# Dealing an expert's ranks to the partitions in steps of eight

## What is computed

```
pg   = softmax(h @ wg);  g_sel = argmax(pg)                 # 4 groups
pf   = softmax of the chosen group's 8 expert logits
top_p, top_i = top_k(pf, 2)                                 # two experts of that group
wts  = max(pg) * top_p / sum(top_p)
out  = sum over the token's two experts of  wts * W_down(silu(W_gate h) * W_up h)
```

## Time and profile before

| | us |
|---|---|
| runs shown | 1400.77, 1408.01, 1413.49 |
| median of the runs | 1408.01 |
| span of the profiled execution | 1406.2 |
| TensorE busy in it | 1299.9 (92%) |
| mean granted TensorE clock | 0.962 |

### The profile page before, as it was taken

How to read it: one execution, slowest core, us unless ns; L and a number is a source line. 1 busy time by engine, 2 the same in 40 slices (tenths; PEclk the granted TensorE clock), 3 DMA queues, 4 the chain that set the end, 5 groups by cost and what they waited for, 6 DMA issues and landing times. The chain is left out here.

```text
span 1406.2 us, 19509 instructions
## 1 busy us (share of the span) xinstructions
PE 1299.9 (92%) x6977; PEld 927.7 (66%) x6977; DVE 743.2 (53%) x1444; ACT 263.0 (19%) x564; POOL 278.5 (20%) x397
## 2 busy tenths in 40 slices
PE   7999999999999999999989888999999799787775
PEld 3787767878778777777777776888878533222224
DVE  1625688998877777100136558675666612111116
ACT  3201112222222443110222213400002300000001
POOL 0223433423334343131200002000002301111000
PEclk9999999999999999999999997999999899999995
DMA  9553233431331334665541113322244599999945
GB/s 362 178 112 113 89 101 120 150 117 64 120 120 60 120 136 141 212 206 166 166 183 35 31 31 136 124 60 90 89 171 193 220 419 419 420 419 420 419 202 200
DMA packets 66594, 250.88 MB, mean 178 GB/s; under 512 B 9834, under 2 KB 21770, under 8 KB 53290
## 3 DMA queue, kind: packets, MB, share of 16 engines
q1 hardware_dynamic: 49858, 213.34, 40.3%
q0 software_dynamic: 10112, 20.47, 4.3%
q10 hardware_dynamic: 6536, 15.90, 3.9%
HBM read 234.47 MB, written 22.91 MB: 183 GB/s over the span
## 5 line engine op out<-in xcount | busy, mean ns | idle before, releaser
L362 PE MATMUL psum<-arena 128*128 128x272 f32 x2408 | 568.9, 394 | 6.4 <-DVE arena L2331 2.0
L362 PEld LDWEIGHTS psum<-arena 128*128 128x128 f32 x2408 | 452.9, 190 | 118.4 <-issue 19.9
L384 POOL TENSOR_TENSOR arena<-arena 128x512 f32<-128x512 f32 x96 | 128.0, 1333 | 202.7 <-DMA arena<-in_weights 158.9
L2840 PE MATMUL psum<-arena 128*64 128x512 f32 x512 | 119.2, 611 | 21.4 <-DMA arena<-in_w_gu 19.0
L1507 PE MATMUL psum<-arena 128*128 128x272 f32 x512 | 121.6, 395 | 0.0
L1507 PEld LDWEIGHTS psum<-arena 128*128 128x128 f32 x512 | 95.3, 189 | 25.1 <-DVE arena L1633 3.6
L2840 PEld LDWEIGHTS psum<-arena 128*64 128x64 f32 x512 | 36.2, 138 | 93.7 <-issue 70.3
L2862 PE MATMUL psum<-arena 128*64 128x512 f32 x256 | 65.1, 654 | 18.9 <-issue 16.2
L2914 DVE TENSOR_TENSOR arena<-arena,psum 128x256 f32<-128x256 f32 x16 | 6.8, 422 | 131.3 <-ACT arena L2905 131.3
L1633 DVE TENSOR_TENSOR arena<-arena,psum 128x272 f32<-128x272 f32 x16 | 7.0, 438 | 128.2 <-ACT arena L1584 128.2
L1827 PE MATMUL psum<-arena 128*128 128x272 f32 x256 | 63.8, 403 | 3.0 <-PEq L206 3.0
(11 more groups left out here) (390 smaller groups left out, 1517.6 us busy)
## 6 DMA issues: line engine op xcount, KB each, us to landing
arena<-in_weights SPq DMA_DIRECT2D x153, 512.0 KB, 4.7
arena<-in_w_gu SPq DMA_DIRECT2D x32, 2048.0 KB, 34.5
arena<-in_w_down SPq DMA_DIRECT2D x16, 2048.0 KB, 34.9
arena<-in_weights ACTq DMA_DIRECT2D x16, 512.0 KB, 4.6
arena<-in_pages_k POOLq DMA_DIRECT2D x40, 128.0 KB, 3.7
arena<-in_x SPq DMA_DIRECT2D x2, 2176.0 KB, 11.9
arena<-in_pages_v SPq DMA_DIRECT2D x32, 128.0 KB, 3.3
arena<-in_pages_v POOLq DMA_DIRECT2D x32, 128.0 KB, 3.5
```

Of the source, the lines that this page charges most:

```text
L362: mm = pe.matmul(out, lhsT=w[:, c * P:c * P + P], rhs=x[:, c, :], start=(c == 0 and not added), stop=(c == 3), skip_group_check=added or more)
L384: link(dve.tensor_tensor(sums[:, k], a, b, op))
L2840: mm = pe.matmul(psum[CAP * e:CAP * e + CAP, 2 + k, :].rearrange("p (o f) -> p o f", o=2), lhsT=xgT[:, k, lo:lo + CAP], rhs=wv[:, e, c4], ...
```

## The change

The slot that a rank gets is no longer the rank itself. The 64 slots are seen as 8 groups (b) of 8 (a), and slot 8b + a gets rank 8a + b: rank 0 goes to partition 0, rank 1 to 8, rank 2 to 16, rank 7 to 56, rank 8 to 1, and so on, in both halves of the partitions. The table of rows, the table of weights and all that follows use the same `slot_of`, so each token still meets its expert. It is one instruction, with another view of its first operand and of its output; it runs once before the pairs and once behind them.

```
+SLOT_STEP = 8
 ...
                 def one_hot_slots():
-                    dve.tensor_tensor(slot_of, const("iota").unsqueeze(1).to_broadcast([P, 2 * NR, CAP]),
-                                      rank.unsqueeze(2).to_broadcast([P, 2 * NR, CAP]),
-                                      ALU.is_equal).then_inc(s_onehot, 1)
+                    spread = const("iota").rearrange("p (a b) -> p b a", b=SLOT_STEP)
+                    of_rank = rank.unsqueeze(2).unsqueeze(3).to_broadcast([P, 2 * NR, SLOT_STEP, CAP // SLOT_STEP])
+                    dve.tensor_tensor(slot_of.rearrange("p k (b a) -> p k b a", b=SLOT_STEP),
+                                      spread.unsqueeze(1).to_broadcast([P, 2 * NR, SLOT_STEP, CAP // SLOT_STEP]),
+                                      of_rank, ALU.is_equal).then_inc(s_onehot, 1)
```

## The result

The changed kernel takes 1417.03 us in the median (1407.76 to 1422.47, 21 runs) against 1408.83 us before (1400.77 to 1415.16, 21 runs). The ratio is 1.0042, 95% interval 1.0026 to 1.0059, so the change costs 3.7 to 8.3 us, 5.9 in the middle. That is less than 1%, but with this many runs it is clear of zero. The ratio rests on all runs; the two medians themselves lie 8.2 us apart, the two means 7.0. The forecast was +5.9 us and a median of 1413.9.

The account below looks back on a forecast made before the run. The expert stage was taken as bound by the DMA engines, ending with the one with the largest share. Rows +5.8 and one-hot instruction +0.1 summed to +5.9 us, median 1408.0 to 1413.9 us; range 1403 to 1422.

Parts of the forecast that it names:

- The bound: Expert stage: bound by the DMA engines at 419 GB/s, not by TensorE; it ends when the engine with the largest share ends.
- Way B: Four neighbouring partitions and the four 32 further on share an engine; largest 189 rows, 10.3 us over mean; chance 0.78.
- A: Rival map, eight neighbouring partitions to an engine: the change evens the load, -13.3 us, 1394.7 us; chance 0.05.
- C: Rival map, partition p to engine p mod 16: the change adds 81 rows, +12.7 us, 1420.7 us; chance 0.04.
- Term (1): Gathers and scatters in the expert stage: fullest engine goes from 189 to 226 rows, 37 x 0.156 = +5.8 us.
- Term (2): Latency of gathers and scatters, including the bare first gather and last scatter: cost 0.
- Term (3): One-hot instruction before the first gather, operand stepping by eight: +0.1 us taken, +0.4 at most; second use 0.
- Term (4): Stage end: both last blocks move with the slowest engine; the clock of one `down` may change 1.6 us either way.
- The plateau near half share: Last 25 to 30 us of the stream: about half the engines at work, DMA share near 0.5, some 210 GB/s.
- the signs of being wrong: End share stays even, light engines' lead feeds back on SP, or the rate before the last 30 us falls below 419.
- the step that no engine runs dry: Weight stream: some 30 us of work stand queued, so an engine works through its whole share without a pause.
- More than the sum: Rival: SP held up by eight full queues, 9.19 us on top of the sum, 1423 us; chance 0.06.

Follow-up runs that it names:

- The even deal: Kernel before, with rank r dealt to group r mod 8, every other turn starting four groups further on: 1401.21 us, ratio 0.9932.
- by table: Kernel before with the change's deal read from a table by the old one-hot instruction: 1415.18 us, ratio 1.0032.
- the other eight: Kernel before with the change's deal, groups swapped in pairs so rows fall on the engines the change leaves nearly empty: 1412.21 us, ratio 1.0027.
- The two kernels without gathers: Kernel before and changed kernel, each with gathers bounded to row 0, scatters kept: 1395.7 us, ratio 0.9890, and 1398.4 us, ratio 0.9909.
- the steepest deal: Kernel before, with eight ranks in a row dealt to four partitions and the four 32 further on before the next group: 1418.04 us, ratio 1.0055.
- the reversed order: Kernel before with rank r dealt to slot 63 - r: 1408.17 us, ratio 0.9988.

## Why the prediction was right, point by point

**The bound.** Right. The stage ends when the fullest DMA engine ends. Seven deals, two of them also without gathers, move the end with the fullest engine's rows, in both directions, and the sum of the rows is the same in all but the two without gathers.

**Which partitions share an engine.** Way B was read from the tail alone: one engine, 10.3 us over the mean. The even deal settles it, since of the three only B makes it even, and its time fell by 6.5 us; A and C fall with it. The Trainium skill, page "DMA: Bandwidth & Descriptors", section "The descriptor swizzle", lists way B for a plain transfer over 128 partitions, and these indirect gathers and scatters agree, with the fullest engine's 143 rows against 189 making 6.5 us. The same page's "Specifications", read as eight neighbours to an engine, would have promised 13.3 us less for the change; 7.6 more were measured in this time (6.5 over the whole stage).

**Term (1), the rows: right in kind, too small.** 37 rows x 0.156 = 5.8 us was forecast, and 7.6 measured (7.3 by table, 6.7 on the other eight). The price of a row was not the fault: leaving rows out gives 0.144 to 0.150. The two kernels without gathers lie 4.1 us apart where 17 rows ask for 2.5, and the steepest deal, with five engines within 4 rows of its maximum, has no such extra. So the deal of the change costs about 1 to 2 us beyond its rows, which is not much more than what kernels of one load differ by (239.2 to 241.0). What it is stays open. The early drop of the stream's rate does not fit it: the changed deal without gathers has the extra and no drop, the fours have the drop and no extra.

**Term (2), latencies: right.** In the changed kernel the gathers land in 11.1 us in the median for 10.6, and TensorE's wait for the first is 1.7 us for 1.6.

**Term (3), the instruction.** Taken at +0.1, bounded at +0.4, measured at +0.47 in three kernels. The value belonged at the upper bound or above: a step of eight numbers was the one thing no row showed, and the row of the same instruction at step one was no evidence for it. Its second use, put at 0, is not quite that: with it the last scatter's instruction is 0.4 us longer.

**Term (4), the tail.** The uncertainty named there, 1.6 us for the clock of one `down`, is what came: 5.29 us before, 3.65 after. The eleven profiles have it at about 5.3 in six and at 3.65 in four; the kernel without gathers in the changed deal has its slow stretch one step earlier, at a gate/up. The quick `down` came to the change's aid here and hid most of the extra in term (1). So the stage's +6.5 is 7.6 less 1.6, plus the half microsecond at the last scatter, and with the instruction the profile has +7.0 for the 5.9 forecast. The ratio's middle, 5.9, equals the forecast by luck as well: three terms were too low and one of unknown sign fell the right way, and the medians are 8.2 us apart.

**The signs named ahead.** The plateau near half share came, at 205 to 217 GB/s, but lasted 16 us, not 25 to 30. The last two blocks are issued by 1343.44 and the light engines are done at about 1352, so their lead was cut by what had been issued; I had put it at the full 30 us. The heavy ones ended within 4 to 6 us. The last block landed at 1374.0 us from the span's start, for 1368.4; 3.5 us of that are the later start. TensorE's wait for gate/up blocks grew from 19.0 to 23.6 us and its idle time before `down` from 16.2 to 20.0, together 8.4 us for the 6 forecast. One of the signs of being wrong came too: the stream's rate before its last 30 us fell below 419, to 388 GB/s from 1280 on. What failed there is the step that no engine runs dry: 395 to 398 GB/s for 75 us is a loss of some 4 us for the mean engine. The full ones cannot have lost as much, since the time is only 1 to 2 us over what their rows ask for; so it fell on the light ones, and cost little.

**More than the sum.** SP was held up more, as that rival had it: its last issues take 9.84 us for 9.19. No 9 us came of it. The lead of the light engines does feed back, as the drop of the rate shows; that it works through SP was not tested.

## What to carry to other kernels

When a stage is bound by the DMA engines, ask for the fullest engine and not for the bytes, and read it from the slope of the DMA share as the stream ends: a slow slide with one engine left alone can be an uneven load, worth at most the distance between the last engine and the mean. A gather or scatter with empty slots in plain order was uneven here, 189 rows on one engine and 69 on another. Another deal of rows to partitions costs next to nothing and can gain, but only by the true map from partition to engine: a deal that would be even for eight neighbours made it worse here by 6 us, and the one for the true map made it better by 9.6, of which 6.5 are rows. Test the map with one deal that only one map makes even, before building on it.

## What was not expected of the hardware

- VectorE reads a float32 operand in steps of eight numbers at 1.30 us for 640 per partition, against 0.83 us in sequence: half again as long. The view had one dimension more as well, and no run tells the two apart.
- Engines far ahead of the others could not use their lead fully here: the light engines of the changed kernel had 29.6 us less to carry (mean of the eight emptier against the eight fuller, 189 rows) and finished 16 to 20 us ahead.
- The start of the expert stage varies by 10 us between executions of programs that are the same up to there (the one-hot instruction begins between 1108.98 and 1118.77 us), more than the whole effect studied. A difference between two spans says little here; differences taken from an event just ahead of the stage repeat to 0.3 us in three kernels of one load (241.0, 240.8 and 240.7 us), and to 1.8 with the reversed order of that load (239.2).
